# Attention of three branches run two couples ahead instead of one, with eight gate tiles among it

## The reference, cut to what matters

```python
n = rmsnorm(h, g_mix)
aq, ak, av, iq, ik, iw, bq, bk, bv, mq = split_cols_2(n @ w_in, IN_SPLITS)
y_a = dsa_attention(rope(aq), rope(ak), av, rope(iq), rope(ik), iw)   # 8 heads
y_b = dilated_attention(rope(bq), rope(bk), bv)                       # 3 groups of 8 heads, one softmax
y_m = memory_attention(mq, rmsnorm(mem, g_mem), w_mem_kv)             # 4 heads, 256 memory rows
gates = sigmoid(n @ w_gate + b_gate)                                  # 3 x 1024
merged = (gates[0] * (y_a @ w_branch[0]) + gates[1] * (y_b @ w_branch[1])
          + gates[2] * (y_m @ w_branch[2]))
h = h + merged @ w_out
h = h + hier_moe(rmsnorm(h, g_ffn), ...)                              # 16 experts, two of one group for each token
```

## Time and profile before

| | |
|---|---|
| median of 3 executions | 1143.7 us (1142.53 to 1145.63) |
| the profiled execution, its own time | 1144.23 us |
| its span, first to last instruction | 1142.3 us |
| mean granted TensorE clock | 0.975 |
| PE busy | 1059.5 us, 93% of the span |
| stage `"abm"`, first scores to last values | 677.74 to 764.74 us of the span |

### The profile page before, as it was taken

One profiled execution on the slowest core, in us unless ns is written; L12 is line 12 of the kernel. 1 busy time (PEld: TensorE's weight loads), 2 busy tenths in 40 slices (PEclk: granted clock), 3 DMA queues, 4 the chain that ended last, 5 costly groups with the idle time before them and its releaser, 6 DMA issues.

```text
span 1142.3 us, 13346 instructions
## 1 busy us (share of the span) xinstructions
PE 1059.5 (93%) x4960; PEld 672.8 (59%) x4960; DVE 401.5 (35%) x1181; ACT 333.3 (29%) x779; POOL 13.8 (1%) x60
## 2 busy tenths in 40 slices
PE   3899999899979998999999999779999999999985
PEld 0344554444457777768888556568888864444432
DVE  2249264332248554622942014651111320100004
ACT  2213133333043345224554024541001321111112
POOL 0000000000000000000000000000000000000010
PEclk9899999999989999999999999998999999999998
DMA  9897217342233212443344342119544769999994
GB/s 368 340 369 256 74 37 307 154 204 74 73 121 138 75 74 82 181 148 114 144 151 157 135 147 75 37 71 427 197 154 154 302 270 419 424 424 424 425 423 194
DMA packets 32909, 238.21 MB, mean 209 GB/s; under 512 B 3696, under 2 KB 3952, under 8 KB 6768
## 3 DMA queue, kind: packets, MB, share of 16 engines
q1 hardware_dynamic: 28192, 200.29, 44.9%
q10 hardware_dynamic: 4080, 34.99, 8.0%
q0 software_dynamic: 576, 2.10, 0.5%
HBM read 232.65 MB, written 19.40 MB: 221 GB/s over the span
## 4 chain that ended last, share of the span: by engine, by line
PE 84%; DMA 6%; ACT 4%; DVE 3%; issue 1%; ACTq 0%; SPq 0%; DVEq 0%
PE lin L447 30%; PE aux L447 9%; PE lin L817 8%; PE lin L529 8%; PE sc L470 6%; PE aux L817 4%; PE aux L731 4%; DMA ring<-w_stream 4%; DMA PR<-w_stream 3%; PE sc L785 3%; PE sc L565 2%; PE lin L578 2%; PE aux L591 2%; PE sc L500 1%; ACT SP L990 1%
## 5 line engine op out<-in xcount | busy, mean ns | idle before, releaser
L447 PE MATMUL lin<-H,ring 128*128 128x256 f32 (+1 forms) x1360 | 342.7, 414 | 5.3 <-ACT H L1031 3.8
L447 PEld LDWEIGHTS lin<-H,ring 128*128 128x128 f32 x1360 | 261.9, 193 | 84.1 <-issue 49.8
L529 PE MATMUL lin<-ring,H 128*128 128x512 f32 (+2 forms) x256 | 90.1, 513 | 0.0
L447 PE MATMUL aux<-Y,ring 128*128 128x512 f32 (+1 forms) x256 | 85.2, 494 | 4.2 <-DVE Y L1406 3.1
L447 PEld LDWEIGHTS aux<-Y,ring 128*128 128x128 f32 x256 | 48.9, 192 | 39.6 <-issue 32.0
L529 PEld LDWEIGHTS lin<-ring,H 128*128 128x128 f32 x256 | 46.3, 190 | 42.7 <-issue 30.1
L980 ACT ACTIVATE SP<-lin 128x512 f32<-128x512 f32 (+3 forms) x96 | 43.8, 467 | 92.7 <-PE lin L578 92.6
L470 PE MATMUL sc<-H,ring 128*128 128x512 f32 (+1 forms) x192 | 70.8, 503 | 0.0
L1354 DVE SCALAR_TENSOR_TENSOR UN<-UN,cols 128x512 f32<-128x512 f32 (+1 forms) x120 | 64.5, 610 | 0.0
L944 ACT ACTIVATE NB<-lin 32x256 f32<-32x256 f32 x168 | 63.0, 375 | 2.6 <-DVE PR L1287 0.6
L990 ACT ACTIVATE SP<-SP,ST 128x513 f32<-128x513 f32 (+5 forms) x88 | 54.7, 621 | 2.4 <-DVE ST L1316 2.2
(11 more groups left out here) (257 smaller groups left out, 1173.9 us busy)
## 6 DMA issues: line engine op xcount, KB each, us to landing
ring<-w_stream SPq DMA_DIRECT2D x127, 1024.0 KB, 5.2
SP<-w_stream SPq DMA_DIRECT2D x12, 1024.0 KB, 24.2
Y<-w_stream SPq DMA_DIRECT2D x8, 1024.0 KB, 17.4
UN<-w_stream SPq DMA_DIRECT2D x8, 1024.0 KB, 22.8
PR<-w_stream SPq DMA_DIRECT2D x8, 1024.0 KB, 26.2
X<-w_stream SPq DMA_DIRECT2D x7, 1024.0 KB, 21.1
CW<-w_stream SPq DMA_DIRECT2D x6, 1024.0 KB, 22.6
H<-w_stream SPq DMA_DIRECT2D x4, 1024.0 KB, 21.4
```

Of the source, the lines that this page charges most:

```text
L447: m = mm(dst, w[:, k, :], rhs(k), start=n == 0, stop=n == KT - 1)
L529: m = mm(bank[:, 0:width], src[:, k, tt * P:(tt + 1) * P], w[k // 4][:, k % 4, 0:width], start=k == 0, stop=k == KT - 1)
```

## The change

- `"abm"` runs with `LAG` 2: turn `p` of PE issues scores `p`, transposes `p - 2`, values `p - 3`. The stage has one turn more, 23 on PE. The mixer layers keep `LAG` 1.
- It has six score buffers: the four of `S` and two in `NB`, which is unused in this stage.
- DVE's turn `p` reads scores `p` first and then scales `p - 1`; before, it scaled first.
- Eight gate tiles are computed inside the stage, six at turns 0, 2, 3, 5, 6 and 8, and two at turns 20 and 21, which have no scores. So the first round behind the stage has four gate tiles, no longer six. The order of the tiles in the weight stream follows.

```diff
+GATE_STEPS = (1, 4, 7, 10, 13, 16, 40, 42)
+EARLY = len(GATE_STEPS)
+LAG = {"l0": 1, "l1": 1, "abm": 2}
...
-        GATE_STEPS = (2, 5, 8, 11, 14, 17)
...
-            return H[:, 1, 2 + 3 * t + b, :] if t < 2 else PR[:, 3 * t + b, :]
+            n = 3 * t + b
+            return H[:, 1, 2 + n, :] if n < 6 else Y[:, 6 + n, :] if n < EARLY else PR[:, n, :]
...
+        def S_of(g):
+
+            n = g - first["abm"]
+            if n < 0:
+                return g % 4, S[:, g % 4, :]
+            n %= 6
+            return n, S[:, n, :] if n < 4 else NB[:, (n - 4) * 772:(n - 3) * 772]
...
-                    if 1 <= p <= n_pairs:
-                        for i in (2 * p - 2, 2 * p - 1):
+                    if lag <= p < n_pairs + lag:
+                        for i in (2 * (p - lag), 2 * (p - lag) + 1):
...
-                    if p >= 2:
-                        pair, g = items[2 * p - 4:2 * p - 2], first[name] + 2 * p - 4
+                    if p > lag:
+                        a = 2 * (p - lag - 1)
+                        pair, g = items[a:a + 2], first[name] + a
...
-                for t in (2 * mp, 2 * mp + 1) if mp else ():
-                    for b in range(3):
-                        gate(t, b)
+                for n in range(max(EARLY, 6 * mp), 6 * mp + 6):
+                    gate(*divmod(n, 3))
...
-            act.wait_ge(lin_taken, turn["gate", 1, 2] + 1)
+            act.wait_ge(lin_taken, turn["gate", *divmod(EARLY - 1, 3)] + 1)
...
+                for p in range(n_pairs + lag + 2):
+                    if lag > 1 and p < n_pairs:
+                        read(p)
                     if 1 <= p <= n_pairs:
-                        g0 = first[name] + 2 * p - 2
...
+                        scaled(p - 1)
+                    if p >= lag + 2:
+                        it = items[2 * (p - lag - 2)]
                         v.tensor_copy(it["to"], take()[:, 0:it["to"].shape[-1]]).then_inc(aux_taken, 1)
...
+                    if lag == 1 and p < n_pairs:
+                        read(p)
```

More of the change, by code:

```diff
@@ L552, in attention @@
             def attention(name, between):
-                items = STAGES[name]
+                items, lag = STAGES[name], LAG[name]
                 n_pairs = len(items) // 2
-                for p in range(n_pairs + 2):
+                for p in range(n_pairs + lag + 1):
                     if p < n_pairs:
@@ L988, in attention @@
                                 lo = 0
[L989 to L991 removed]
+                            n, buf = S_of(g)
+                            e = buf[:, lo:1 + it["w"]]
+                            fn(e, e, ACT.Exp, bias=ST[:, n, 1:2], scale=it["scale"],
+                               accum_out=ST[:, n, 2:3]).then_inc(probs_ready, 1)
                     between(2 * p + 1)
@@ L1289, in attention @@
             def attention(name, between=lambda i: None):
-                items = STAGES[name]
+                items, lag = STAGES[name], LAG[name]
                 n_pairs = len(items) // 2
-                for p in range(n_pairs + 3):
-                    if 1 <= p <= n_pairs:
-                        g0 = first[name] + 2 * p - 2
[L1295 to L1303, removed]
-                        v.tensor_copy(it["to"], take()[:, 0:it["to"].shape[-1]]).then_inc(aux_taken, 1)
[L1305 to L1316, removed]
@@ new lines, in scaled @@
+                def scaled(p):
+                    g0 = first[name] + 2 * p
+                    for g in (g0, g0 + 1):
+                        st = ST[:, S_of(g)[0], :]
+                        dve.wait_ge(probs_ready, g + 1)
+                        n = step(v.reciprocal(st[:, 3:4], st[:, 2:3]))
+                    for x, g in enumerate((g0, g0 + 1)):
+                        after(n - 1 + x)
+                        b, buf = S_of(g)
+                        e = buf[:, 1:1 + items[2 * p + x]["w"]]
+                        v.tensor_scalar(e, e, ST[:, b, 3:4], None, ALU.mult).then_inc(probs_scaled, 1)
@@ new lines, in read @@
+                def read(p):
+                    for i in (2 * p, 2 * p + 1):
+                        it, s, g = items[i], scored_first[name] + i, first[name] + i
+                        held = 6 if name == "abm" else 4
+                        if i >= held or g >= held and name != "abm":
+                            dve.wait_ge(lin_ready, T_LAST[g - held] + 1)
+                        dve.wait_ge(scores_ready, s + 1)
+                        b, buf = S_of(g)
+                        w, st = it["w"], ST[:, b, :]
+                        most = SK[:, it["sink"]:it["sink"] + 1] if it["sink"] is not None else -3e38
+                        v.tensor_tensor_reduce(out=buf[:, 1:1 + w], in0=sc[:, s % 2, 0:w], in1=it["mask"], scale=1.0,
+                                               scalar=most, op0=ALU.add, op1=ALU.max, accum_out=st[:, 0:1]).then_inc(scores_taken, 1)
+                        dve.wait_ge(scores_taken, s + 1)
+                        v.tensor_scalar(st[:, 1:2], st[:, 0:1], -it["scale"], None, ALU.mult).then_inc(bias_ready, 1)
@@ L1732 @@
     for mp in range(4):
-        stream += [gates[b * KT + t][None] for t in (2 * mp, 2 * mp + 1) for b in range(3)]
+        stream += [gates[n % 3 * KT + n // 3][None] for n in (range(max(6 * mp, EARLY), 6 * mp + 6) if mp else range(EARLY))]
         stream += [branches[b][mp][None] for b in range(3)]
```

18 lines of the change are left out of this document (10 added, 8 removed).

## The result

| | changed | before |
|---|---|---|
| median, executions | 1134.97 us, 6 (1130.59 to 1135.87) | 1143.12 us, 6 (1139.99 to 1145.63) |
| ratio of the times | 0.9926, 95% interval 0.9906 to 0.9946 | |
| the profiled execution, its own time | 1130.59 us | 1144.23 us |
| its span; granted clock | 1128.8 us; 0.983 | 1142.3 us; 0.975 |

The change is 8.2 us faster at the medians, 0.74%. The forecast was 1137.6 us, 6.1 us less.

A forecast was written before the change was run, and what follows sets the result against it. It took PE's timeline up to the experts as the path, with the end's transfer queue shifting along. Waits out 9.9, new waits 3.6 and tiles 0.2 left 6.1 us: 1137.6 us, own range 1136.0 to 1139.8, wider 1134.9 to 1140.7.

The forecast's parts named there:

- What goes: PE's waits in stage `abm`: 7.8 us for scaled probabilities and 2.1 us for scores read go, 9.9 us out.
- What stays: Stage `abm`: four bank waits of 0.62 us at wide couples and 1.3 us at three gate tiles remain.
- What comes: Stage `abm`: new PE waits, mostly for scores read at couples 2 and 10 and two end tiles, 3.6 us.
- The rival on the score slots: Branch b: with one couple in `sc`, PE waits for every wide read; gain only 2.5 us, 1141.2 us; chance 0.11.
- Two tiles moved: Two gate tiles moved from behind the stage into it cost 0.11 us more each, 0.2 us.
- The sum: Whole kernel: 9.9 - 3.6 - 0.2 = 6.1 us gained; bounds 9.7 and 2.5 us.
- The clock: Stage `abm`: short waits cost no clock by the long-gap rule and the trace, so the 6.1 us stay unchanged.
- Behind the stage: First branch blocks: PE's 3.87 us stall and the half clock after it, 2.7 us lost, stay as they are.
- The rival that the clock's fall there shrinks: Behind the stage's stall: the half clock goes or shrinks; gain 6.1 + 2.7 us, 1134.9 us; chance 0.09.
- The transfers at the end: Kernel's end: last loads bound by something earlier than PE's frees do not move; time stays 1143.7 us; chance 0.05.
- The ring: Gate tiles behind the stage, needed sooner, run short during the expert loads; PE waits, 1165 us; chance 0.02.

The follow-up runs named there:

- again: The changed kernel timed again with no edit, against the kernel before in the same session: 1133.39 us against 1144.26, ratio 0.991.
- the first experiments' session: Batch of runs on one chip for the four experiments that take the change apart; the kernel before has a median of 1144.89 us there.
- one couple ahead, new tiles: The changed kernel with `LAG` 1 in the stage, so DVE scales first again, and its eight gate tiles kept: 1141.91 us, ratio 0.9975.
- filled waits: The kernel before plus four extra constant matmuls ahead of the transposes in each of turns 10, 12, 14 and 16: 1143.52 us, ratio 0.9991.
- the one with the larger `ST`: The kernel before with only the scratch tile `ST` enlarged by 32 bytes a partition, as in the change: 1145.1 us, ratio 1.0005.
- the scaling first: The changed kernel, still two couples ahead, with DVE scaling before it reads the new scores: 1137.47 us, ratio 0.9929.
- The experiment with the sigmoids first: The changed kernel with ACT's eight sigmoids ahead of its wait for the last values and the eleven loads: 1128.09 us, ratio 0.9858.

## Why the prediction was right in its waits and short in its time

**What goes: right.** All eight waits for the scaling are gone. The table of waits predicted 9.9 us out.

**What stays: right.** Four times 0.62 us and 1.3 us at the three tiles, to the digit. So of the two repeating gaps that the Trainium skill's *Perfetto Trace Analysis*, "Optimization Strategy", can lay to a short buffer, only the 0.62 us one is one here; the 1.20 us did not come back at another buffer.

**What comes: right in sum and place.** Scores 2 took 1.05 us for 1.2, scores 10 1.33 for 1.3, scores 8 0.26 for 0.2; scores 11 and the transposes of couple 2 nothing new; the two end tiles 0.7 for 0.7: 3.3 us for 3.6. The rival on the score slots is out: PE waits at the first wide couple only. It takes both the read order and the six buffers for that; with either left out the waits for scores are 6.6 or 4.5 us instead of 2.6.

**Two tiles moved: nothing instead of 0.2 us.** The one at 752.19 us takes 3.46 us to the next start (755.65), as much as behind the stage; the other one too.

**The sum: 6.1 us forecast, 7.3 in the pair of profiles.** From the first scores to the routing it is 225.55 before and 218.22 after. Idle time is 6.5 of it, where I had 6.3. The number of waits in the stage went from 19 to 13, and at 0.07 us beyond the row each that is 0.4. The rest, 0.4 us, I can't assign.

**The clock: the step that failed.** "By that rule, and with the trace, short waits as in the stage cost no clock", so the rule "leaves the 6.1 us as they are": the sum had no term for the clock. The row for it was the window 730 to 740 us at 1.00, and I took it for a property of the kernel. It was one of that execution: in the same program, with the same waits, two later executions ran at half the clock twice each in branch b, and their stage lasted 90.66 and 91.92 us instead of 87.53 (in the latter 1.7 us are the fall in branch a). The Trainium skill's page *TensorE: Matmul & The Clock Gate* has a case of this from another kernel, in "A second HAM failure mode: psum-queue depth-cycling": short idle times of PE between groups of matmuls, as PSUM banks are cycled, can be frequent enough that the clock goes back and forth. I had weighed only its rule on long gaps. The traces fit: the place is a 1.20 us wait for data and a 0.62 us wait for a bank, and twelve products there run at half the speed.

How much of the gain is this? For each execution I split the span into its part at full clock (span times granted clock) and the rest. Means:

| | executions | at full clock | lost to the clock |
|---|---|---|---|
| before, the session of "again" | 17 | 1114.5 | 27.7 |
| before, the first experiments' session | 13 | 1113.9 | 29.3 |
| changed | 6 | 1107.8 | 24.5 |
| changed, again | 6 | 1107.6 | 24.0 |
| one couple ahead, new tiles, the first experiments' session | 10 | 1113.4 | 26.7 |
| filled waits | 12 | 1114.0 | 26.6 |
| before, its session | 17 | 1113.8 | 27.7 |

The part at full clock shrinks by 6.9 us on the chip of "again", 6.3 against the other before; that is the predicted part, within its error of under 1 us. The time lost to the clock shrinks by 3.7 there, and this I had left out. With all 12 executions of the change and all 47 of before it is 3.9, with a standard error of 1.1.

Where is it lost? The four profiles of before and of the one with the larger `ST` have a stage 2.7 us longer on average than 87.53, at the same waits. That alone could account for most of it. But summed over windows of 4 us, the profiles show as large a difference ahead of the stage, where the work is identical. All five profiles with the program of before (with the filled waits) lose 11.9 to 18.8 us there, 15.7 on average. The nine with the changed program, `LAG` 1 among them, lose 8.6 to 17.1, on average 12.3; the difference has a standard error of 1.5. In the first pair it is nearly everything: 17.1 us before and 8.6 after, so the stage starts 5.6 us earlier. The profile on which I predicted lost 28.5 us in all, as the executions of before do in the mean. Its stage had no fall, but its time was no low base.

That the clock is where the rest of the gain came from is shown by the split. That the removed waits in branch b are its cause is not shown, and the rival that the part ahead of the stage runs with fewer falls in the changed program stays open. For the waits: of the eight profiles with two couples ahead (the change twice and six variants) seven have no fall in branch b, and that of the eighth stands behind a 1.59 us wait; of the five with one couple ahead and nothing in the waits four have one or two. Against them: with the waits filled the clock's loss is 1.1 us less, no more than could be chance with a standard error of 1.5. With `LAG` 1 and the new tiles, where 5.8 us of the waits for the scaling are left, it is 2.6 less than before in its session (standard error 1.0). And with the scaling first the stage has 11.59 us of idle time and no fall. The stage also starts anywhere between 672 and 678 us, with identical work ahead of it, and what the clock does there differs from execution to execution by as much as is in question here.

**Behind the stage: right.** The stall took 3.90 us and the half clock came again. The rival that the clock's fall there shrinks has the measured time, 1134.9, but not by its mechanism: the fall did not shrink, others did. The experiment with the sigmoids first shows what the stall and its fall are worth: 6.8 us, close to the 6.6 worked out from the earlier trace rows (3.87 and 2.7).

**The other rivals.** The transfers at the end moved with PE: the last load landed 11.9 us earlier, the span is 13.5 us shorter (5.6 of that lay before the stage already). The ring never ran short: in 660 to 775 us PE waits for no transfer.

## What to carry to other kernels

A row of a single profile tells what an instruction waits for, and that holds from execution to execution, mostly to 0.01 us here; what the clock did in it does not. Before a sum goes against a time, look at the granted clock of all executions and split the time into the part at full clock and the loss. When waits of about a microsecond are to be removed from PE, give the clock a term or a rival of its own in the forecast, and the range room to that side: here the clock's part was over a third of the gain.

To run two couples ahead takes three things at once: the distance, buffers for one couple more, and the consumer's order (free the producer's slot first). With the order or the buffers missing the way to the routing is 3.8 us longer here, about half of the 7.3 gained (with the buffers missing, 1.7 of it is the clock's in that profile). And look at the stall at the stage's end: moving eight sigmoids ahead of eleven load instructions was worth nearly as much to the routing as the whole reordering, 6.8 against 7.3 us.

## What the runs showed of the hardware

- Waits as short as 1.20 and 0.62 us, close to each other, were followed by 1.2 GHz in four of five profiles and in one they were not. Two falls made the stage 3.1 us longer (90.66 and 90.67 for 87.53), about 1.6 us each.
- A stall of 3.8 to 4.2 us was followed by the half clock in all twelve profiles that had it. The 32 products behind it took 8.83 to 10.17 us instead of 7.0, so it cost 1.8 to 3.2 us on top of itself, 2.9 in the changed kernel.
- A wait costs 0.07 us more than its row shows, since matmuls that follow without a wait start ahead of the modelled end of the one before.
- A load instruction on ACT's queue takes about 0.5 us of ACT's time; eleven of them and the table load (1.28 us) held the first sigmoid for 7 us, from the last values at 758.6 us to 765.60. In the changed kernel ACT's rows there are the following; the 7.04 us in brackets begin earlier, with ACT's last copy, and count the issuing as idle.

```profile
758.61 0.34 ACTq L1120 DMA_DIRECT2D MORE<-w_stream  x1
758.97 0.94 ACTq L1120 DMA_DIRECT2D UN<-w_stream  x2
...
764.31 1.28 ACT L1126 ACT_TABLE_LOAD   x1 [7.04 <-issue]
765.60 2.50 ACT L1126 ACTIVATE H<-H,cols 128x256 f32<-128x256 f32 x6
```
